# A hybrid decoder layer with product-key experts: the first chunk's end by tiles, and the first head's experts in two halves

## The reference

```python
x1 = x + gt1 * (merged @ w_out)
h2 = modulate(rmsnorm(x1, g_norm2), sh2, sc2)
q = (h2 @ w_pq).reshape(n, 8, 2, 128)
s = einsum('nhsd,hskd->nhsk', q, sub_keys)
sv, si = top_k(s, 16)
cand = (sv[:, :, 0, :, None] + sv[:, :, 1, None, :]).reshape(n, 8, 256)
cidx = (si[:, :, 0, :, None] * 128 + si[:, :, 1, None, :]).reshape(n, 8, 256)
fv, fp = top_k(cand, 16)
eidx = take_along_axis(cidx, fp); g = softmax(fv)
act = gelu(einsum('cd,ced->ce', h2, u_tab[eidx]))
x2 = x1 + gt2 * einsum('ce,ced->cd', g * act, v_tab[eidx])
```

## Time and profile before

| what | value |
| --- | --- |
| median of three runs | 1971.66 us |
| lowest, highest | 1970.85, 1972.91 us |
| the profiled execution's own time | 1972.74 us |
| its span | 1970.4 us |
| busy: TensorE, VectorE, ScalarE, POOL | 1358.7, 1257.7, 597.6, 1098.4 us |
| granted clock of TensorE, mean | 0.802 |
| moved by DMA | 701.87 MB, mean 356 GB/s |
| gathers of U and of V | 520 and 520 |

### The profile page before, as it was taken

How to read it: one execution, slowest core, us unless ns; L and a number is a source line. 1 busy time by engine, 2 the same in 40 slices (tenths; PEclk the granted TensorE clock), 3 DMA queues, 4 the chain that set the end, 5 groups by cost and what they waited for, 6 DMA issues and landing times.

```text
span 1970.4 us, 23769 instructions
## 1 busy us (share of the span) xinstructions
PE 1358.7 (69%) x7318; PEld 864.6 (44%) x7318; DVE 1257.7 (64%) x3101; ACT 597.6 (30%) x1657; POOL 1098.4 (56%) x1062
## 2 busy tenths in 40 slices
PE   6998999857888678989877876444443444544444
PEld 5887799845655444667555553111110111111111
DVE  3265436477777888867778856666667666666640
ACT  2446424233344255322223432112212112211110
POOL 0100010166666477766855767777777776677764
PEclk8999999979989889888898897656566655666567
DMA  9755245599999899999999999999999999999997
GB/s 362 258 186 212 97 156 201 196 374 409 409 408 384 329 373 360 403 410 385 409 405 392 406 409 403 409 404 403 407 408 402 404 403 404 367 409 407 402 396 288
DMA packets 202447, 701.87 MB, mean 356 GB/s; under 512 B 22569, under 2 KB 32369, under 8 KB 202033
## 3 DMA queue, kind: packets, MB, share of 16 engines
q0 software_dynamic: 149760, 545.33, 70.1%
q1 hardware_dynamic: 52560, 155.02, 21.6%
HBM read 691.26 MB, written 11.06 MB: 356 GB/s over the span
## 4 chain that ended last, share of the span: by engine, by line
DMA 20%; issue 13%; PE 12%; POOL 11%; DVE 9%; ACT 2%; POOLq 0%; DVEq 0%; SPq 0%; ACTq 0%
DMA arena<-in_v_tab,pku 13%; POOL arena L2196 11%; PE y L1171 6%; DMA arena<-in_u_tab,pku 6%; DVE arena L2021 4%; PE acc L806 4%; DMA arena<-in_xT 1%; ACT arena L1264 1%; DVE pku L2042 1%; PE acc L946 1%; DVE arena L1753 0%; PE turned L1151 0%; DVE pk L2041 0%; DVE pk L2057 0%; DVE pku L2058 0%
## 5 line engine op out<-in xcount | busy, mean ns | idle before, releaser
L2196 POOL DMA_INDIRECT arena<-in_u_tab,pku x520 | 550.9, 1060 | 356.9 <-issue 150.5
L1171 PE MATMUL y<-arena 128*32 128x512 f32 x2080 | 411.5, 907 | 467.2 <-DMA arena<-in_v_tab,pku 467.2
L2196 POOL DMA_INDIRECT arena<-in_v_tab,pku x520 | 532.4, 1024 | 255.5 <-issue 148.2
L806 PE MATMUL acc<-arena 128*128 128x264 f32 (+1 forms) x2304 | 556.4, 400 | 18.6 <-ACT arena L1308 8.1
L806 PEld LDWEIGHTS acc<-arena 128*128 128x128 f32 x2304 | 451.0, 199 | 128.2 <-issue 53.5
L2021 DVE CUSTOM_DVE_ANT_0 arena<-arena,h_bank 128x1024 f32<-128x1024 f32 x240 | 291.0, 1219 | 252.3 <-DMA arena<-in_u_tab,pku 251.8
L1171 PEld LDWEIGHTS y<-arena 128*32 128x32 f32 x2080 | 82.7, 143 | 710.7 <-issue 703.4
L2021 DVE CUSTOM_DVE_ANT_0 arena<-arena 128x1024 f32<-128x1024 f32 x280 | 335.1, 1222 | 83.4 <-DMA arena<-in_u_tab,pku 68.4
L1507 ACT ACTIVATE pk<-pk 128x1 f32<-128x1 f32 x520 | 103.6, 281 | 2.1
L1529 ACT CAST pku<-turned 128x8 uint32<-128x8 f32 x64 | 10.4, 162 | 283.8 <-PE turned L1151 256.9
L2239 POOL TENSOR_TENSOR o_lo<-arena,o_hi 128x256 fp32r<-128x256 f32 x8 | 6.6, 863 | 156.8 <-ACT o_hi L1383 156.8
(11 more groups left out here) (249 smaller groups left out, 1822.7 us busy)
## 6 DMA issues: line engine op xcount, KB each, us to landing
arena<-w_mod SPq DMA_DIRECT2D x48, 512.0 KB, 5.5
arena<-w_pq SPq DMA_DIRECT2D x32, 512.0 KB, 6.9
arena<-w_xr SPq DMA_DIRECT2D x20, 512.0 KB, 8.2
arena<-w_qk SPq DMA_DIRECT2D x20, 512.0 KB, 7.7
arena<-w_gr SPq DMA_DIRECT2D x20, 512.0 KB, 6.9
arena<-w_rnn SPq DMA_DIRECT2D x16, 640.0 KB, 6.6
arena<-in_u_tab,pku POOLq DMA_INDIRECT x520, 8.2
arena<-in_v_tab,pku POOLq DMA_INDIRECT x520, 7.5
```

What stands on the lines that cost most here:

```text
L806: mm = pe.matmul(a[:, 0:n], w[:, k, :], rhs[:, k, 0:n], start=(k == 0), stop=(k == ks - 1))
L1171: mm = pe.matmul(y[rows, h, :], spread[g % NTURN][:, 32 * j:32 * j + 32], rows_v[j][:, h * 512:(h + 1) * 512], start=first and (g != SAMPL ...
L2196: pool.indirect_dma_start(out=row, out_offset=None, in_=table, in_offset=bass.IndirectOffsetOnAxis(ap=idx, axis=0), **more).then_inc(signa ...
```

## The change

**By tiles.** For chunk 0, `scale_tiles` on VectorE takes the reciprocal and scales x1 by gain and norm in one operation per 128 columns, tile 0 first; ScalarE's `shift_rows` adds the shift. `pqa` 0 and 1 are query columns 0 and 1 for tile 0, `first` follows, and `pqb` 0 and 1 are the same columns for tile 1. The order after the norm is now: `pqa`, `first`, `rowsh` of tile 0, `mod` 10 and 11, `pqb`, `rowsh` of tile 1, `pq` 2 and 3, `keys` of the first pair, `rowsx`, `modT` 10 and 11, `pq` 4 and so on.

**Eight experts first.** `first_names` ranks only eight of either half, adds them to 64 sums, takes the best eight and computes their numbers straight into `eidx[0]`; POOL's first group waits for `s_first` instead of `s_idx`. Then the full ranking of head 0 goes on, and `number(0)` fills the second eight.

**Second head.** ScalarE copies head 1's scores of tile 0 from PSUM to `stage[1]` beside the spill copy; SP no longer reads them back. Its `RANK_FROM` is 0 instead of 2.

**Spills and ring.** Chunk 0 has seven spill places, chunk 1 three. The ring of 11 places is used for all pieces up to `pq` 7 and `keys` of the second pair, and the five places from `pq` 8 on.

```diff
@@ _plan, the order
-        mods(ch, "norm")
-        for i in range(2 * (CT + ch)):
+        if ch == 0:
+            for c in range(2):
+                product(0, "pqa", c, (("pq", c),), 1.8)
+            product(0, "first", 0, (("keys", 0),), 0.5)
+            for i in range(2):
+                product(0, "rowsh", i, (), 0.2)
+            mods(0, "gains")
+            for c in range(2):
+                product(0, "pqb", c, (("pq", c),), 0.3)
+            for i in range(2, 4):
+                product(0, "rowsh", i, (), 0.2)
...
@@ _slots
-        late = int(FIRST[p] >= PEER_FROM)
-        if p == (0, "keys", 0):
-            place[1] = place[0] % (OWN + EXTRA) + 1
+        late = int(FIRST[p] >= NO[0, "pq", 8])
+        if not late:
+            place[1] = (place[0] + 1) % (OWN + EXTRA)
...
-RANK_FROM = [PARTS * g - 2 * PARTS + 2 * int(h in (1, 2)) for h, g in enumerate(FIRST_GROUP)]
+RANK_FROM = [PARTS * g - 2 * PARTS + 2 * int(h == 2) for h, g in enumerate(FIRST_GROUP)]
...
-NSPILL = 3
+NSPILL = (7, 3)
...
@@ SP
-                if k in STAGE_AT[1:]:
-                    load_stage(STAGE_AT.index(k, 1))
+                if k in STAGE_AT[2:]:
+                    load_stage(STAGE_AT.index(k, 2))
...
@@ TensorE
+            def project_tile(name, c, t):
+
+                w = await_piece(pe, (0, "pq", c))[:, 0:D].rearrange("p (k m) -> p k m", k=DC)
+                a = take(0, name, c)
+                for k in range(DC):
+                    if c == 0:
+                        if t == 0:
+                            pe.wait_ge(s_h, DC + k + 1)
+                        else:
+                            pe.wait_ge(s_hb, k + 1)
+                    mm = pe.matmul(a[:, 0:P], w[:, k, :], h2T[:, k, t * P:(t + 1) * P], start=(k == 0), stop=(k == DC - 1))
                 mm.then_inc(s_ready, 1)
...
@@ ScalarE
+            def shift_rows(t, cs):
+
+                for c in cs:
+                    act.wait_ge(s_scaled, DC * t + c + 1)
+                    rows = h2T[:, c, t * P:(t + 1) * P]
+                    act.activation(rows, rows, ACT.Identity, bias=mod[:, 3 * DC + c, 0:1]).then_inc(s_hb if t else s_h, 1)
...
+                ins = act.copy(spill[SPILL_SLOT[k]][0:rows, :], a[0:rows, :])
+                if (ch, name, i) == (0, "keys", 0):
+                    ins = act.copy(stage[1], a[:, 2 * NKEYS:4 * NKEYS])
+                release(ins, ch, name, i)
...
+                if ch == 0:
+                    shift_rows(0, range(DC))
+                    yield NO[0, "pqa", 0]
+                    query_tile("pqa", 0, 0)
+                    shift_rows(1, range(4))
+                    yield NO[0, "pqa", 1]
+                    query_tile("pqa", 1, 0)
+                    yield NO[0, "first", 0]
+                    a = take(0, "first", 0)
+                    release(act.copy(stage[0], a[:, 0:2 * NKEYS]), 0, "first", 0)
+                    shift_rows(1, range(4, DC))
...
             course.until(PEER_FROM)
+            course.until(NO[0, "pqb", 0] + 1)
             spread_keys(0)
+            course.until(NO[0, "pq", 2] + 1)
+            number(0)
             exponentials(0)
-            number(0)
...
@@ VectorE
+            def scale_tiles():
+
+                await_read(dve, 0, "norm", 1)
+                for t in range(CT):
+                    cols = slice(t * P, (t + 1) * P)
+                    link(dve.reciprocal(rstd2[:, cols], rstd2[:, cols]))
+                    for c in range(DC):
+                        dve.scalar_tensor_tensor(h2T[:, c, cols], x1[:, c, cols], mod[:, 4 * DC + c, 0:1], rstd2[:, cols],
+                                                 ALU.mult, ALU.mult).then_inc(s_scaled, 1)
...
+            def first_names():
+
+                await_read(dve, 0, "first", 0)
+                for half in range(2):
+                    x, b = stage[0][:, half * NKEYS:(half + 1) * NKEYS], best[:, half, 0:SLOT]
+                    rank(dve.max(b, x))
+                    rank(dve.max_index(keyi[:, 16 * half:16 * half + SLOT], b, x))
+                rank(dve.tensor_copy(keyq, keyi.rearrange("p (s k) -> p s k", s=2)[:, :, 0:SLOT]))
+                few = cand[:, 0:SLOT * SLOT]
+                rank(dve.tensor_tensor(few.rearrange("p (i j) -> p i j", i=SLOT), best[:, 0, 0:SLOT].unsqueeze(2).to_broadcast([P, SLOT, SLOT]),
+                                       best[:, 1, 0:SLOT].unsqueeze(1).to_broadcast([P, SLOT, SLOT]), ALU.add))
+                rank(dve.max(fv[:, 0:SLOT], few))
+                rank(dve.max_index(posi[:, 0:SLOT], fv[:, 0:SLOT], few))
+                dve.tensor_scalar(pos2[:, 0:SLOT], posi[:, 0:SLOT], 3, None, ALU.logical_shift_right)
+                rank(dve.tensor_scalar(pos2[:, SLOT:2 * SLOT], posi[:, 0:SLOT], SLOT - 1, None, ALU.bitwise_and))
+                rank(dve.tensor_copy(placeq, pos2[:, 0:2 * SLOT]))
...
+                rank(dve.tensor_reduce(pickq, hot, AX.X, ALU.add))
+                dve.scalar_tensor_tensor(eidx[0][:, 0:SLOT], pickq[:, 0:SLOT], float(NKEYS), pickq[:, SLOT:2 * SLOT],
+                                         ALU.mult, ALU.add).then_inc(s_first, 1)
...
@@ POOL
+                    elif g == 0:
+                        pool.wait_ge(s_first, 1)
```

More of the change, by code:

```diff
@@ L118, in mods @@
         for what, i in MODS.get(place, ()) if ch == 0 else ():
-            product(0, what, i, tuple(("mod", 4 * i + q) for q in range(4)) if what == "mod" else (), 4.0 if what == "mod" else 0.5)
+            product(0, what, i, tuple(("mod", 4 * i + q) for q in range(4)) if what == "mod" else (), (0.5 if place == "gains" else 4.0) if what == "mod" else 0.5)
     def block(ch, name, c):
@@ L949, in sample_product, with token_rows @@
                 mm.then_inc(s_ready, 1)
-            def token_rows(ch, name, src):
-                for i in range(2 * (CT + ch)):
+            def token_rows(ch, name, src, first=0, last=2 * (CT + 1)):
+                for i in range(first, min(last, 2 * (CT + ch))):
                     t, h = divmod(i, 2)
```

187 lines of the change are left out of this document (120 added, 67 removed).

## The result

**It became slower.** Over 20 runs of each kernel the changed kernel has a median of 1978.76 us (1972.94 to 1987.51) and the kernel before 1972.66 us. The medians are 6.1 us apart; the estimate of the ratio is 1.0024, 95% interval 1.0013 to 1.0034, some 5 us. 1965.2 was forecast, with 1958.0 to 1972.5 as the range. The profiled execution took 1980.35 us, its span is 1978.4 us, so against the span of before (1970.4) the trace has 8.0 us to account for.

A forecast was written before the change was run, and what follows sets the result against it. It took the kernel as bound by DMA bytes once expert gathers begin. Idle DMA time falls from 19.1 to 13.0 us, 6.4 saved with the dropped read-back: 1972.7 to 1966.3, median 1.1 below, 1965.2 us; range 1958 to 1972.5.

The forecast's parts named there:

- parts (1) and (2): Chain to the first gather: ranking begins at 365.9 instead of 373.40, first gather at 370.9 to 371, 12.7 us earlier.
- Part (3): Rest of head 0: all names at 381.8, POOL hardly waits, first dot product at 384.2 instead of 388.65.
- Part (4): Second head straight to its ranking: its first gather at 403.5 to 404 instead of 417.62.
- Parts (5) and (6): Stores and query weights, 3.15 MB, move behind the first gather; stores issue without a wait, first V gather at 412.
- the sum: Idle DMA time from 356 to 440 us: 13.0 against 19.1, 6.1 us less, 6.4 with 128 KB not read back.
- 0.5 for 416 to 440: Last term of idle DMA time: 0.5 us between 416 and 440 us, where 3.1 stood before.
- rival C: Slower: earlier second-chunk products hold dot products from 620 to 760 us, idle nearly doubles by 12 us, 1977.2; chance 0.08.
- its sign (below 0.87): DMA share from 620 to 760 us falling below 0.87 would show rival C.
- Rival A: The 12.7 us lead at the first gather is carried whole, since weight loads have slack: 1959; chance 0.14.
- B: Gather 9's wait moves behind query column 2, number(0) at 389, 6.2 us idle instead of 1.5: 1971; chance 0.20.
- The wait for V's places behind `keys` 3: First V gather must wait for keys 3 instead of pq 1; done by 411, before POOL arrives at 412.

The follow-up runs named there:

- Experiment 8: Single parts undone; for the ranking, `norm_and_chunk1_old_quarters` with head 1 ranked two quarters later again, as before: ratio 0.9980 beside 0.9978.
- norm_step_later_chunk1_old_quarters: Changed kernel with VectorE's norm step two quarters later, score read-back first in its quarter, old quarters from the second chunk's first xr product: 0.9961, median 1965.73 us.
- norm_and_chunk1_old_quarters: Changed kernel with the old kernel's quarters from the second chunk's first norm on, that norm in quarter 11 instead of 9: 0.9978, median 1968.25 us.
- late_after_pq5_true_cost: Changed kernel with the last two modulations behind query column 5 and their plan cost 3.8 each instead of 0.5: 0.9971, median 1966.43 us.
- second_head_late_again: `norm_and_chunk1_old_quarters` with head 1 ranked in quarters 4 to 6 again, its scores still straight from PSUM: 0.9980.
- best_with_ring_undone: `old_quarters_and_late_after_pq5` with the choice of weight ring as before the change: 0.9980 beside 0.9963.
- old_quarters_and_late_after_pq5: `norm_and_chunk1_old_quarters` with the last two modulations moved behind query column 5: 0.9963, 1966.06 us.
- both_repairs_stage_first: `old_quarters_and_late_after_pq5` with the score read-back issued first in its quarter: 0.9971.
- no_eight_first: `old_quarters_and_late_after_pq5` with head 0 fully ranked to 16 before any gather: 0.9986 beside 0.9963.

## Why the prediction was wrong

**The chain to the first gather, parts (1) and (2): right but for one term.** From VectorE's reciprocal to its first maximum it was 14.5 us and is 365.29 - 356.82 = 8.5, where the working had 7.0: TensorE's 16 matrix products (32 records) take 5.26 us, not 4.0. The 4.0 came from a row at full clock, and here the granted clock is 0.53 from 358.6 to 362 us, nearly all at 1.2 GHz, after 2.54 us in which TensorE stood idle; the same 16 products for the second tile, at 369.28 and a granted clock of 1.00, take 3.84 us. From that maximum to the names 4.15 us, 4.2 forecast; POOL 1.0 later. The gather at 370.39 met the forecast of 371, but by luck: the chain was 1.5 us longer than I had it, and a reciprocal that began 2.1 us earlier than in the trace of before made up for it. That is no effect of the change, since it began between 355.3 and 357.6 in all later traces, whatever the order.

**Part (3): right in size, with a wait missed.** Gather nine waited 1.6 us and the first dot product came at 383.41 (384.2 forecast). But VectorE then waited 4.07 us for the last modulations, which now stand behind `pq` 3 and `keys`; gathers 11 and 12 came at 390.97 and 395.66, each behind a wait for its place. I named what ScalarE and POOL are queued behind, and not this for VectorE.

**Part (4): 3 us late, and without a value that shows.** Head 1's first gather came at 406.92, where 403.5 to 404 was forecast; the names were ready at 404.9, behind the 4.07 us just named, and the gather stood behind the last one of head 0, which had waited for its place. Experiment 8 shows no gain from the earlier ranking.

**Parts (5) and (6): issues as forecast** (371.36, 387.83, stores at 386.85 and 391.61). The first V gather came at 418.10, not 412. It did not wait for TensorE or for a place: POOL's seven gathers from 406.92 on took 11.2 us, up to 2.3 each, where I had reckoned 1.24 each, and they began 3 us late.

**The step that failed** is the last term of the sum, "0.5 for 416 to 440", together with the silence on 440 to 620 us. The first was 3.5 us, by the norm in quarter 9. The second was put at nothing, without a reason, and measured 8.4 us: 389 GB/s for 408, and in the lead table the way from -1.1 at k = 12 to +6.0 at k = 42, of which 4.1 fall between 36 and 39. The front matter of this text tells that the planner's quarters move; the prediction priced that only as rival C, in the stretch 620 to 760 us. I looked for the collision where the share was already low and missed that a stretch at share 1.03 has the more to lose, and that one moved product, the norm, has a long chain back to VectorE (squares 2.6 us, sum 6.67, root 0.48). An engine that waits in order for such a chain needs its own other work queued ahead; in quarter 9 the dot products that POOL needed stood behind it.

**Rival C had the mechanism of one of the two losses, in the wrong place.** Its 12 us were set for 620 to 760 us, where the share went from 0.93 only to 0.92, so its sign (below 0.87) did not come. The collision was at k = 36 to 39, 587 to 618 us in the kernel that shows it best, and cost 8 to 9.5 us of lead there and 4.1 in the changed kernel, whose lead was gone by then. The wait for the norm was in no rival. That C's 1977.2 lies near the measured 1978.76 is luck. C got 0.08; what the two cliffs ask for is a chance of their own for each moved consumer on VectorE.

**The sum, once the quarters were put right.** In `norm_step_later_chunk1_old_quarters` the idle time is 9.6 + 1.9 + 1.5 + 0 = 13.0 us (shares 0.32, 0.90, 0.97 and 1.03 in its four windows), as forecast for the change, and by the ratio it is 7.7 us shorter than the kernel before (4.9 to 10.5, six runs), where 6.4 were forecast. So this part of the working holds within its noise. That its median of 1965.73 us is 0.5 from the 1965.2 forecast is partly luck: the kernel before had 1973.54 in the same series, and the trace with those 13.0 us is of the slowest of its six runs, 1971.54 us, only 1.2 below the profiled run of before.

Rival A fell: of a first lead of 12 to 14 us, 7 are left at k = 36, and 10.5 us is the most that the interval allows. B fell too: the names behind query column 2 kept gather nine for 1.6 us, where B had the names at 389. The wait for V's places behind `keys` 3 never showed. The Trainium skill (Trainium Kernel Development and Optimization, Key Constraints) says that DMAs of all issuing engines run on the same 16 engines and interleave. The trace agrees: from 386 to 416 us SP's moved weights and POOL's gathers go through one share of 1.01. No run here tells how much of the shrinking lead (13.2 at k = 0, 10.7 at k = 8) is theirs, since VectorE's wait of 4.07 us has a part in it.

**Where the later lead goes.** In five traces of kernels with the old quarters (`norm_and_chunk1_old_quarters`, the best `norm_step_later_chunk1_old_quarters`, `late_after_pq5_true_cost`, `second_head_late_again` and `best_with_ring_undone`) 4.1 us of it go between k = 82 and 86. In `old_quarters_and_late_after_pq5`, `both_repairs_stage_first` and `no_eight_first` nothing goes there. The five have a hole in the transfers from 890 to 900 us (share 0.66 to 0.71), and ahead of it TensorE stood idle for 4.0 to 7.7 us before a product at 865 to 867 us, with a granted clock of 0.56 to 0.76 from 860 to 870. The three have a share of 1.02 or 1.03 from 890 to 900, no such idle time and a granted clock of 1.00. The best kernel first, then `old_quarters_and_late_after_pq5`:

```profile
860.00:870.00 10.00, 4.53 (x12) 3.63 (x13) 9.51 (x26) 1.04 (x4) 4.82 (x5) 0.56 1.02 409
890.00:900.00 10.00, 10.00 (x36) 8.17 (x36) 5.29 (x11) 0.76 (x2) 5.29 (x6) 0.74 0.71 249
```

```profile
860.00:870.00 10.00, 8.47 (x39) 6.69 (x37) 9.51 (x26) 1.34 (x5) 4.77 (x5) 1.00 1.03 411
890.00:900.00 10.00, 10.00 (x52) 7.12 (x51) 4.93 (x10) 1.08 (x3) 6.87 (x6) 0.97 1.03 410
```

Whether the clock causes the hole is not shown, nor whether a kernel falls on the same side in each run: the best kernel's trace is its slowest run.

## What to carry to other kernels

- Where a planner turns costs into places, a small change of a cost is a part of the change like any other. Compare the resulting order line by line, and for each step that moves ask which engine consumes it, how long its chain is, and whether that engine has other work ahead of it.
- Try an edit of the order by itself on the old kernel: here the order alone cost 0.40%, while the edits that were meant gained 0.2 to 0.4% with the old order or nearly so.
- A stretch with full queues is not safe; it has the most to lose. Two waits of VectorE of 9 to 10 us, some 20 us apart, were worth quite different things: taking the one for the read-back away changed nothing that the runs can tell, and taking the one for the norm away, while no place was free, gave 0.26%, some 5 us.

## What the runs showed of the hardware

The sum of the norm's squares takes 6.67 us in the changed kernel and 4.84 us in `norm_and_chunk1_old_quarters`, for the same eight matrix products (16 records). The windows of 417 to 424 us, of the one and of the other, show the granted clock (the number ahead of the DMA share):

```profile
417.00:424.00 7.00, 6.59 (x17) 5.20 (x18) 0.00 (x0) 1.59 (x2) 3.60 (x4) 0.56 1.04 416
```

```profile
417.00:424.00 7.00, 7.00 (x26) 5.82 (x27) 4.10 (x7) 4.46 (x16) 5.78 (x5) 0.76 1.03 414
```

A clock of 0.56 is nearly all of the stretch at the lower level, 1.2 GHz, and 0.76 half of it at 2.4 GHz. TensorE had been idle for 3.23 us right ahead of the sum in the changed kernel, and for 2.34 us ahead of the records before it in the other. So by this comparison up to 1.8 us of the 10.13 us wait are the clock's. It is no condition of the loss: in `norm_step_later_chunk1_old_quarters` the sum takes 6.82 us as well (granted clock 0.53 in the same window), and VectorE waits 0.45 us for the root. No run set the clock by itself.
